# Two weight copies placed ahead of the small steps of a unit in ScalarE's queue

## The chip, the cores and the metric

The kernel runs on one core of a Trainium2 chip, in one launch. The metric is the device time of that core in microseconds. Three timed executions of the kernel before took 2869.0, 2869.91 and 2870.35 us; the median is 2869.91 us. PE is TensorE (PEld its weight loads), ACT is ScalarE, DVE is VectorE, POOL is GpSimd, SP is SyncE, which issues the weight DMAs.

## The reference

Two layers run one after the other over 256 tokens of width 2048, all in float32. The first takes 16 meta tokens ahead of them. It is a normed input projection, stick-breaking attention with 8 heads, a pool over trailing windows of 2, 4, 8 and 16 tokens, two gated projections back to 2048, and an output projection. The second is a hybrid mixer (chunked retention with 8 heads, gated delta rule with 16 heads), cross attention to 256 memory tokens, and a feed-forward block of width 8192.

```
h = rmsnorm(x); zin = h @ w_in                       # 2048 x 10240
y = sigmoid(m_attn) * (o_attn @ w_attn_up) + sigmoid(m_pool) * (o_pool @ w_pool_up)
x = rmsnorm(x + y @ w_out)
x = x + hybrid_mixer(rms_norm(x))                    # conv of 4 taps, silu, l2 norm, delta rule
x = x + cross_attention(rms_norm(x), rms_norm(mem))
x = x + square(relu(rms_norm(x) @ w_ff1)) @ w_ff2
```

For a pair of delta-rule heads the mixer projects queries, keys and values, runs a convolution of four taps over the tokens, applies silu, scales queries and keys to length one, inverts a triangular matrix of 64 by 64 per chunk, and passes a state through the chunks.

## The kernel before, in words

**Units.** All weights lie in one array of 471 units of 128 x 2048 floats (1 MB each; some are shorter). A unit passes three stations. SP loads it into one of three raw buffers. ACT copies it, rounded to float32r, into one of three `whi` buffers. DVE subtracts the copy from the raw weights into one of three `wlo` buffers. TensorE multiplies high part and low part with the likewise split activations. Copy and subtraction are made in two halves, (j, 0) and (j, 1), and so are the unit's matmuls, `("mm", (j, 0))` and `("mm", (j, 1))`. A high copy of unit j waits for the raw load, and for `w_used` of unit j - 3, that is for the last matmul of the unit that held the same `whi` buffer (`s_hi`, line 1698; the copy is line 1704). The subtraction is `s_lo` (line 2068, by the helper in line 2042). Every matmul stands in line 1346 (line 1349 the transposes), so that one goes by tiles in the trace.

**The written order.** `make_plan` writes one list of steps; each engine's program walks it and emits the steps that it has a part in, in the list's order. So the list is the order of each engine's queue, and an instruction that waits holds up all behind it on its engine. `hi_to(n)`, `lo_to(n)` and `load_to(n)` add high copies, low parts and loads up to unit n if they are not in the list yet. `SPL` and `RAW` are 3.

**A unit's steps.** `unit()` (line 236) adds, for unit j: low parts of the next units and the high copies of unit j + 2 where they are missing; the first half's matmuls; a `slot()` where the stage has `half=True`; a low half; the second half's matmuls; the reading of a finished sum (`last()`, where a pair of units ends); a `slot()`; and the second low half of unit j + 2. The high copies of unit j + 3 come at the start of the next call, so behind the slot at the end of unit j. A unit that is `lazy`, the last before the input of the matmuls changes, leaves its last low half to the next.

**Slots.** `slot()` moves every running task by one step. The tasks are generators: attention heads (`g_att`), norm factors of the second layer (`g_factors`, line 611), retention heads (`g_ret`, `g_rtr`), convolutions (`g_conv`, line 756), delta-rule head pairs (`g_gdn`, line 796), cross attention (`g_x`), transposes (`g_xt`). A step has parts on several engines. Those that the prediction speaks of are:

- `cvs`: ACT makes the sigmoid of a convolution's result (line 1900); DVE multiplies with it in `cvq`; ACT squares the product (line 1905) and rounds the square to `cacc_r` (line 1907).
- `cvl`: DVE makes the low part `t` of the squares. `cvn`: TensorE sums both over the head, `cacc_r` first, then `t`; ACT takes Ln and Exp of the sum (`rsqrt`, lines 1739 and 1741).
- `g_up` and `g_down`, five times by turns for block sizes 2 to 32: TensorE multiplies, DVE copies to `Cm`; TensorE multiplies, ACT copies to `TT` (line 1929), DVE transposes `TT` to `Tn` (line 2556). `g_up64` and `g_down64` end the inversion. `g_v` and `g_o` follow, with DVE copying to `U` (line 2613).
- `a2`: ACT copies and DVE subtracts the merged activations for the output projection of the first layer (lines 1795 and 2042). They stand between two units.
- `mixf`, `fin tok`, `fin n1`: a TensorE sum, Ln and Exp on ACT (two functions, each with its table load), and four DVE operations.
- `att_z`, `att_e`, `att_o`: the attention scores, the weights (an Exp on ACT, line 1777, and then masks on POOL, line 2784), and the product with the values.

In the delta-rule stage a slot stands in the middle and at the end of each unit. One head pair has 10 units: two each for queries, keys and values, and four for a gate. The inversion of pair h runs beside the convolutions of pair h + 1. For pairs 1 to 7 `g_down` falls in the middle of units and `g_up` at their ends. Pair 0 has one `yield` more (`if h == 0: yield`), and there `g_down` falls at the ends and `g_up` in the middle.

Of the kernel before, what the change touches and what calls it, by code (L numbers as in the profile page):

```python
# [161 lines left out]
class Plan:  # L162
# [9 lines left out]
    def add(self, stage, key, **values):  # L172
        self.steps.append((stage, key))
        self.at[stage, key] = values
        return values


RAW, SPL = 3, 3
# [3 lines left out]
def make_plan():  # L182
# [8 lines left out]
    def load_to(n):  # L191
        while done["load"] < min(n, len(units)):
            j = done["load"]
            done["load"] += 1
            add("load", j)

    def hi_to(n):
        while done["hi"] < min(n, len(units)):
            j = done["hi"]
            done["hi"] += 1  # L200
            load_to(j + 1)
            for k in range(2):
                add("hi", (j, k))

    def lo_to(n):
        while done["lo"] < min(n, 2 * len(units)):
            j, k = divmod(done["lo"], 2)
            done["lo"] += 1
            hi_to(j + 1)
            add("lo", (j, k))  # L210
            if k == 1:
                load_to(j + 1 + RAW)
# [3 lines left out]
    def slot():  # L216
        for g in list(tasks):
            if next(g, "end") == "end":
                tasks.remove(g)
# [16 lines left out]
    def unit(half=False, hooks={}, lazy=False, first=None, last=None):  # L236
        j = done["unit"]
        done["unit"] += 1
        lo_to(2 * (j + SPL - 1))
        hi_to(j + SPL)  # L240
        if (j, 0) in hooks:
            hooks[j, 0]()
        add("mm", (j, 0))
        if (j, 1) in hooks:
            hooks[j, 1]()
        if half:
            slot()
        lo_to(2 * (j + SPL) - 1)
        add("mm", (j, 1))
        if first:  # L250
            first()
        if last:
            last()
        slot()
        if not lazy:
            lo_to(2 * (j + SPL))
# [5 lines left out]
    def pair(kind, tag, ready, evac, half=False, lazy=False, hooks={}, defer=False):  # L262
        p = begin(kind, tag, ready)
        full = done["unit"] + p["nu"]

        def read():
            name, value = evac(tag, p["idx"], p["bank"], full)
            main.free(p["bank"], name, value)

        for k in range(p["nu"]):  # L270
            end = k == p["nu"] - 1
            unit(half, hooks, lazy and end, read_late if k == 0 else None, (lambda: waiting.append(read)) if end and defer else read if end else None)

    def turns(kind, two, ready, half=False, hooks={}):

        ps = [(begin(kind, tag, ready), evac) for tag, evac in two]
        full = done["unit"] + 3

        def read(n):
            def f():  # L280
                p, evac = ps[n]
                name, value = evac(p["tag"], p["idx"], p["bank"], full + n)
                main.free(p["bank"], name, value)
            return f

        for k in range(4):
            unit(half, hooks, first=read_late if k == 0 else None, last=read(k - 2) if k > 1 else None)
# [2673 lines left out]
```

## Time and profile before

| | |
|---|---|
| median of 3 executions | 2869.91 us (2869.0 to 2870.35) |
| profiled execution, span from first to last instruction | 2866.7 us |
| PE busy | 2829.8 us (99%) |
| DVE busy | 1931.7 us (67%) |
| ACT busy | 1355.2 us (47%) |
| POOL busy | 57.2 us (2%) |
| granted TensorE clock, mean | 0.999 |
| HBM read | 499.95 MB, 175 GB/s |

The profiled execution is known by its span; what the device time has beside a span is the 3.2 us between 2866.7 and the median. A busy time adds the durations of an engine's instructions without counting an overlap twice. The ends of matmuls are modelled, so that an idle time of PE is the least that it can have been.

### The profile page before, as it was taken

To read this page: it belongs to the slowest core of one execution; us is meant where nothing else is said; L and a number is where in the kernel's file an instruction comes from. 1 tells how busy PE (TensorE), PEld (TensorE's weight loads), DVE (VectorE), ACT (ScalarE), POOL (GpSimd) and SP (SyncE) were. 2 spreads that over 40 slices of the span, in tenths; PEclk is the share of its full clock that TensorE was granted. 3 is DMA by queue.
4 is the path that set the end of the run, shared out by engine and by line. 5 is a ranking of instruction groups with operands and counts; after the bars stand their busy time and mean duration, and the time that the engine had idled before them with its cause. 6 is when DMAs were issued, how large, how long until landed. Compare 5 with 4: busy or idle time off the path is not lost.

```text
span 2866.7 us, 38752 instructions
## 1 busy us (share of the span) xinstructions
PE 2829.8 (99%) x15872; PEld 2442.7 (85%) x15872; DVE 1931.7 (67%) x2513; ACT 1355.2 (47%) x1729; POOL 57.2 (2%) x102
## 2 busy tenths in 40 slices
PE   9999999999999999999999999999999999999998
PEld 8899888888888888888888888888888888888887
DVE  7645557678766658888888875456666655566556
ACT  5433654357443446555555543444345434444434
POOL 0000210000000000000000000000000000000000
PEclk9999999999999999999999999999999999999999
DMA  7444444564555544334343455544354454554453
GB/s 278 183 184 162 143 166 185 197 231 177 197 184 193 204 151 162 141 139 147 133 145 123 145 175 192 187 182 162 146 200 182 178 204 182 200 200 182 186 196 147
DMA packets 72849, 506.66 MB, mean 177 GB/s; under 512 B 8384, under 2 KB 8512, under 8 KB 12896
## 3 DMA queue, kind: packets, MB, share of 16 engines
q1 hardware_dynamic: 71136, 497.83, 46.9%
q0 software_dynamic: 1104, 5.90, 0.6%
q8 instruction: 126, 2.06, 0.3%
q10 hardware_dynamic: 432, 0.45, 0.0%
q14 instruction: 51, 0.42, 0.0%
HBM read 499.95 MB, written 2.10 MB: 175 GB/s over the span
## 4 chain that ended last, share of the span: by engine, by line
PE 86%; DVE 9%; ACT 3%; issue 2%; DMA 1%; SPq 0%; DVEq 0%; POOL 0%; ACTq 0%
PE double L1346 80%; PE bank L1346 5%; DVE cacc L2048 2%; DVE wlo L2042 2%; ACT whi L1704 1%; DVE cst L2065 1%; PE bank L1349 1%; DVE cacc L2045 1%; ACT L1900 0%; DVE Tn L2556 0%; DVE cst L2042 0%; DVE Cm L2042 0%; ACT tmp L1905 0%; DMA vec<-in_vec 0%; DMA raw<-in_wall 0%
## 5 line engine op out<-in xcount | busy, mean ns | idle before, releaser
L1346 PE MATMUL double<-AA,whi 128*128 128x512 f32 (+1 forms) x5008 | 1643.1, 380 | 3.5 <-DVE wlo L2042 3.3
L1346 PE MATMUL double<-AA,wlo 128*128 128x256 f32 (+1 forms) x4624 | 1297.0, 281 | 0.0
L1704 ACT ACTIVATE whi<-raw 128x1024 fp32r<-128x1024 f32 x926 | 925.2, 1049 | 780.3 <-PE double L1346 748.5
L2042 DVE TENSOR_TENSOR wlo<-raw,whi 128x1024 fp32r<-128x1024 f32 (+1 forms) x934 | 1101.7, 1214 | 229.9 <-ACT whi L1704 227.6
L1346 PEld LDWEIGHTS double<-AA,whi 128*128 128x128 f32 x5008 | 915.9, 188 | 181.2 <-DVE wlo L2042 5.2
L1346 PEld LDWEIGHTS double<-AA,wlo 128*128 128x128 f32 x4624 | 874.7, 189 | 1.5
L1346 PE MATMUL double<-whi,AA 128*128 128x512 f32 x1536 | 487.9, 393 | 0.5 <-DVE wlo L2042 0.5
L1346 PEld LDWEIGHTS double<-whi,AA 128*128 128x128 f32 x1536 | 288.5, 188 | 61.0 <-DVE wlo L2042 1.3
L1346 PE MATMUL double<-whi,BB 128*128 128x512 f32 x1024 | 316.8, 389 | 0.0
L1346 PE MATMUL double<-wlo,AA 128*128 128x512 f32 x768 | 299.1, 389 | 0.0
L1346 PEld LDWEIGHTS double<-whi,BB 128*128 128x128 f32 x1024 | 192.2, 188 | 40.1
L1346 PE MATMUL double<-wlo,BB 128*128 128x512 f32 x512 | 199.3, 389 | 0.0
L1346 PEld LDWEIGHTS double<-wlo,AA 128*128 128x128 f32 x768 | 144.4, 188 | 28.7
L2065 DVE TENSOR_REDUCE tmp<-double 128x512 f32<-128x1024 f32 x60 | 73.4, 1224 | 133.1 <-PE double L1346 133.1
L1346 PEld LDWEIGHTS double<-wlo,BB 128*128 128x128 f32 x512 | 96.1, 188 | 19.8
L2042 DVE TENSOR_TENSOR XT<-double,XT 128x512 f32<-128x512 f32 x64 | 41.3, 686 | 93.0 <-PE double L1346 93.0
L1980 ACT ACTIVATE tmp<-tmp 128x512 f32<-128x512 f32 x32 | 20.2, 633 | 172.1 <-DVE tmp L2048 172.1
L1346 PE MATMUL double<-BB,whi 128*128 128x512 f32 x256 | 90.0, 394 | 0.0
L2048 DVE SCALAR_TENSOR_TENSOR cacc<-cst,vec,cacc 128x256 f32<-128x256 f32 x144 | 69.8, 485 | 5.1
L1346 PE MATMUL double<-BB,wlo 128*128 128x256 f32 x256 | 71.6, 280 | 0.0
L2042 DVE TENSOR_TENSOR X<-double,X 128x512 f32<-128x512 f32 x48 | 33.2, 691 | 53.4 <-PE double L1346 52.5
L2042 DVE TENSOR_TENSOR BB<-tmp,BB 128x512 fp32r<-128x512 f32 x40 | 27.7, 693 | 49.5 <-ACT BB L1753 49.5
(335 smaller groups left out, 1722.2 us busy)
## 6 DMA issues: line engine op xcount, KB each, us to landing
raw<-in_wall SPq DMA_DIRECT2D x462, 1024.0 KB, 4.8
raw<-in_wall SPq DMA_DIRECT2D x9, 256.0 KB, 6.7
X<-in_xT SPq DMA_DIRECT2D x1, 2048.0 KB, 11.4
Mm<-in_memT POOLq DMA_DIRECT2D x1, 2048.0 KB, 15.5
tmp<-rqk POOLq DMA_DIRECT2D x16, 128.0 KB, 2.2
mblk<-in_memT SPq DMA_DIRECT2D x8, 256.0 KB, 4.5
dec<-in_dec POOLq DMA_DIRECT2D x1, 1536.0 KB, 8.6
hs<-in_hsT SPq DMA_DIRECT2D x4, 272.0 KB, 5.2
```

The costliest lines, as they stand in the source:

```text
L1346: return q.matmul(out, lhsT, rhs, start=start, stop=stop, skip_group_check=True)
L1349: return q.transpose(out, in_, C("ident") if ident is None else ident)
L1704: q.activation(hi_of(j)[:, c], raw[j % RAW][:, c], ACT.Copy).then_inc(S("w_hi"), 1)
L1980: q.activation(x, x, ACT.Square).then_inc(S("f_act"), 1)
L2042: return q.tensor_tensor(out, a, b, o)
L2045: return q.tensor_scalar(out, a, s, None, o)
L2048: return q.scalar_tensor_tensor(out=out, in0=a, scalar=s, in1=b, op0=o0, op1=o1)
L2065: q.reduce_sum(out, both, mybir.AxisListType.X).then_inc(S("sum"), 1)
```

## The change

In `unit()`, for all but the lazy units, the high copies of unit j + 3 are now written ahead of the slot at the end of unit j, behind the reading of a finished sum. Before, they were written behind this slot, at the start of the next unit's call. Nothing is added to or taken from any engine, and no wait changes its target.

```
--- before.py
+++ after.py
@@ -251,6 +251,8 @@
             first()
         if last:
             last()
+        if not lazy:
+            hi_to(j + 1 + SPL)
         slot()
         if not lazy:
             lo_to(2 * (j + SPL))
```

## Rows read from the trace of the kernel before

**Rows 1.** The page's busy line: busy us, share, instructions.
```profile
PE 2829.8 (99%) x15872; PEld 2442.7 (85%) x15872; DVE 1931.7 (67%) x2513; ACT 1355.2 (47%) x1729; POOL 57.2 (2%) x102
```
**Rows 2.** Windows: stretch, its us, busy (instructions) of PE, PEld, DVE, ACT, POOL.
```profile
1180.00:1650.00 470.00, 457.48 (x2804) 382.05 (x2804) 400.04 (x683) 250.63 (x378) 16.18 (x21) 1.00 0.39 139
...
2190.00:2857.00 667.00, 667.00 (x3375) 569.93 (x3374) 398.55 (x404) 282.24 (x318) 0.00 (x0) 1.00 0.49 186
```
**Rows 3.** Timeline of ACT, queries' convolution: start, us, instruction, idle and releaser.
```profile
1453.87 0.64 ACT L1900 ACTIVATE tmp<-cacc 128x512 f32<-128x512 f32 x1 [3.72 <-DVE cacc L2048]
1456.17 0.63 ACT L1905 ACTIVATE tmp<-qkvq 128x512 f32<-128x512 f32 x1 [1.67 <-DVE qkvq L2042]
1456.83 0.63 ACT L1907 ACTIVATE cacc_r<-tmp 128x512 fp32r<-128x512 f32 x1
1457.37 1.99 ACT L1704 ACTIVATE whi<-raw 128x1024 fp32r<-128x1024 f32 x2
1459.27 0.55 ACT L1929 ACTIVATE TT<-bank 64x128 f32<-64x128 f32 x2
```
**Rows 4.** Timeline of DVE in the same head pair.
```profile
1459.85 0.91 DVE L2556 STREAM_TRANSPOSE Tn<-TT 64x256 f32<-64x256 f32 x2 [2.58 <-ACT TT L1929]
...
1475.13 0.67 DVE L2042 TENSOR_TENSOR t<-tmp,cacc_r 128x512 fp32r<-128x512 f32 x1
1476.06 1.23 DVE L2042 TENSOR_TENSOR wlo<-raw,whi 128x1024 fp32r<-128x1024 f32 x1 [0.26 <-ACT whi L1704]
...
1486.77 0.41 DVE L2613 COPY U<-bank 128x256 f32<-128x256 f32 x1
```
**Rows 5.** Timeline of ACT, keys' convolution of that pair.
```profile
1471.03 1.28 ACT L1900 ACT_TABLE_LOAD   x1 [4.64 <-DVE cacc L2048]
1472.32 0.63 ACT L1900 ACTIVATE tmp<-cacc 128x512 f32<-128x512 f32 x1
1473.78 0.63 ACT L1905 ACTIVATE tmp<-qkvk 128x512 f32<-128x512 f32 x1 [0.83 <-DVE qkvk L2042]
```
**Rows 6.** Timeline of PE where that pair's delta rule goes on.
```profile
1487.33 0.46 PE L1346 MATMUL bank<-U,cross 128*128 128x128 f32 x2 [0.60 <-DVE U L2613]
```
**Rows 7.** Timeline of ACT beside the inversion of head pair 0.
```profile
1152.32 0.63 ACT L1900 ACTIVATE tmp<-cacc 128x512 f32<-128x512 f32 x1 [5.26 <-DVE cacc L2048]
1152.86 0.55 ACT L1929 ACTIVATE TT<-bank 64x128 f32<-64x128 f32 x2
...
1169.34 0.55 ACT L1929 ACTIVATE TT<-bank 64x128 f32<-64x128 f32 x2
```
**Rows 8.** Timeline of PE: the end of the inversion of head pair 0.
```profile
1170.03 0.65 PE L1346 MATMUL bank<-TT,Mf 64*64 64x64 f32 x8 [0.67 <-ACT TT L1929]
```
**Rows 9.** Timeline of PE: the norm sum of pair 0's keys.
```profile
1103.32 0.47 PE L1346 MATMUL bank<-cacc_r,ones_r 128*128 128x512 f32 x1 [1.48 <-ACT cacc_r L1907]
```
**Rows 10.** Timeline at the second layer's start, ACT: Exp of `fin n1`.
```profile
708.42 0.42 ACT L1741 ACTIVATE rs__123<-rs__123 128x256 f32<-128x256 f32 x1
```
**Rows 11.** The same stretch, DVE: first operation of `fin n1`.
```profile
709.01 0.42 DVE L2099 TENSOR_SCALAR nacc__124<-bank 128x256 f32<-128x256 f32 x1
```
**Rows 12.** The same stretch, PE: second half of unit 116.
```profile
712.91 0.50 PE L1346 MATMUL double<-whi,AA 128*128 128x512 f32 x1 [0.52 <-DVE wlo L2042]
```
**Rows 13.** Timeline at the first layer's output projection, ACT: seven `a2` copies.
```profile
592.22 3.75 ACT L1795 ACTIVATE AA<-Macc 128x512 fp32r<-128x512 f32 x7
```
**Rows 14.** The same stretch, DVE: seven `a2` low parts.
```profile
592.86 4.30 DVE L2042 TENSOR_TENSOR AA<-Macc,AA 128x512 fp32r<-128x512 f32 x7
```
**Rows 15.** The same stretch, PE: the output projection's first matmul.
```profile
594.97 0.39 PE L1346 MATMUL double<-AA,whi 128*128 128x512 f32 x1
```
**Rows 16.** Timeline of POOL: attention weights masked; three of eight lie like this one.
```profile
332.47 0.69 POOL L2784 TENSOR_SCALAR_AFFINE_SELECT att<-att 128x128 f32<-128x128 f32 x3 [9.64 <-ACT att L1777]
```
**Rows 17.** Timeline of PE: the product with the values that waits for them.
```profile
335.73 0.97 PE L1346 MATMUL bank<-att,v 128*128 128x256 f32 x6
```

More of the change, by code:

```diff
@@ L253, in unit @@
             last()
+        if not lazy:
+            hi_to(j + 1 + SPL)
         slot()
```

## The prediction

> **What bounds the kernel now.** I read the page's busy line first: TensorE is busy 2829.8 of 2866.7 us, no other engine over 67% [rows 1]. A change of order on ScalarE can therefore only give back TensorE's 36.9 us of idle time, or add to it. So I looked for where they lie, with windows by stage. The feed-forward stage has none: TensorE is busy 667.00 of 667.00 us [rows 2]. The delta-rule stretch from 1180 to 1650 us holds 12.5 (470.00 less 457.48) [rows 2]; the rest is at the kernel's start and end and in a handful of places at changes of stage. Then I went through the waits of TensorE and the timelines of the delta-rule stretch. Each of the six head pairs whose convolutions (of pairs 2 to 7) run beside an inversion shows the same five late places in the side steps: the operand `TT` of `g_up`, `t` of `cvn`, `Cm`, `Ce`, and `U` of `g_o`, the last one with 0.60 us idle [rows 6]. What is late there is VectorE: from the reading of the queries' sum to that copy of `U` it has no pause but one of 2.58 us, where it waits for ScalarE's `TT` [rows 4], and some under 0.7 us. ScalarE is slow with `TT` because it stands behind a pair of high copies, and these behind the square and the rounding of `cvq` [rows 3]. In this stretch the order on ScalarE decides, though it is busy only about half of the time.
>
> **The change part by part.** The edit moves a pair of high copies; it adds no instruction. The two copies hold ScalarE for 1.90 us (1457.37 to 1459.27, when the next begins) [rows 3]. Its DMAs stay where they are: `hi_to` asks for a load that the list already has, so nothing moves past SP's queue, and POOL's has no part in it. The copy's own wait, for the last matmul of unit j, is met about when the slot begins, so what is queued behind it (the end-of-unit steps on ScalarE, and VectorE and TensorE that wait for these) is late by at most the 1.90 us, unless a table load had stood hidden in an idle stretch. At most unit ends ScalarE has no step between the two places: there nothing changes, and that is the whole feed-forward stage after its first units, the memory keys and nearly all of the output projections.
>
> *Head pairs with conv 2 to 7, six times.* Now the sigmoid starts at 1453.87, the square waits for VectorE until 1456.17, and the copies follow behind both. With the change the copies follow the sigmoid (next instruction 0.54 behind a start, as from 1456.83 to 1457.37): 1454.41 to 1456.31. The square then starts at 1456.31, the rounding 0.66 later, `TT` at 1457.51 in place of 1459.27 [rows 3]. The copies use a pause, and VectorE goes on 1.76 us earlier. In the keys' convolution the same move costs: the sigmoid would start 1.76 earlier, at 1470.56, the copies run from 1471.10 to 1473.00, and the square starts at 1473.00, 0.78 earlier than now [rows 5]; so does the rounding, and `t` on VectorE, 1474.35 for 1475.13. Behind it the low part no longer waits 0.26 for its high copy (its start lies 0.93 behind that of `t`; I take 0.61 without the wait, with some launch time): 1474.96 for 1476.06 [rows 4]. From there to the copy to `U` at 1486.77 VectorE has no pause, so `U` and TensorE's `g_o` come 1.10 earlier [rows 4, 6]. Gain 6 x 1.10 = 6.6 us. Bounds: 0, if the keys' part takes all back, and 6 x 1.76 = 10.6, if it takes nothing; 12.5 is all the idle time [rows 2]. I take 1.10, which is chained from adjacent rows.
>
> *Head pair 0, inversion beside conv 1.* Here `g_down` falls at ends of units, so its `TT` copies come behind the moved copies. At 1152.86 `TT` stands directly behind the sigmoid [rows 7]; it gets 1.90 us later, and VectorE, with no pause until the last `TT`, with it. Two `TT` before it lose 1 us each in idle stretches of VectorE and leave about 0.3 (estimate from the same timeline). At 1169.34 the same happens again: the sigmoid is late by 2.2, and the copies come in between: 1.90 more [rows 7]. TensorE takes that `TT` at 1170.03 with 0.67 idle already [rows 8], so it passes all of it on: 0.3 + 1.90 + 1.90 = +4.1 us. Bounds: 1.9 (only the last one counts) and 4.1.
>
> *Conv 0, no inversion beside it.* The square now starts 1.46 us behind the sigmoid's start [rows 5]; with copies between, 0.54 + 1.90 = 2.44. Each `cacc_r` is 0.98 later. The queries' delay passes on some 0.7 (less the 0.26 for the low part), the keys' adds 0.98: +1.7. TensorE already waits 1.48 us for the keys' `cacc_r` [rows 9], so it is paid in full. Bounds 1.0 and 2.0.
>
> *Start of the second layer.* `fin n1` stands at the end of unit 114: its Exp ends at 708.84 [rows 10] and VectorE takes it up at 709.01 [rows 11]. With the copies of unit 117 ahead it ends at 710.74; VectorE starts at 710.78, 1.77 later, and the low part behind it is the one that TensorE waits for at 712.91 with 0.52 idle [rows 12]. So +1.8. `mixf` one unit before is late by as much, but VectorE then waits for `fin tok` anyway, whose end doesn't move. Bounds 0 and 1.8.
>
> *First layer's output projection.* The seven `a2` copies begin at 592.22 [rows 13] and would begin at 594.12. The first low part, now 592.86 and one seventh of 4.30 long, so ready by 593.55 with its tail [rows 14], would be ready at 595.45, with some 0.1 to the matmul 595.55; TensorE wants it at 594.97 [rows 15]. +0.6. Bounds 0 and 1.0.
>
> Sum: 0.6 + 1.8 + 1.7 + 4.1 - 6.6 = +1.6 us on the profiled 2866.7. The median lies 3.2 above this span; I carry the difference over: 2869.91 + 1.6 = 2871.5 us.
>
> *What the rest hides.* The attention weights of three heads come 1.9 later: masked by 333.16 now [rows 16], by 335.06 then, and TensorE takes them at 335.73 [rows 17], 0.67 left. In the other heads a table load that now runs in an idle stretch would come behind the copies, and the delay stays under that. The norm factors of cross attention and feed-forward come up to 2.6 us later (1.9, and part of a table load that is now hidden), with VectorE's low parts behind them still a few tenths before their matmuls. If that cover is too thin, it is a few tenths at each.
>
> One page speaks against the change. The row shows a table load of 1.28 us and the sigmoid 1.29 behind the load's start [rows 5]: nothing else is paid. The Trainium skill ("ScalarE: Activation LUTs", What ACT_TABLE_LOAD costs) states that a switch costs about 2.66 us, since a drain of 1.38 comes with the load. By that, copies that are now put directly ahead of table loads would make those dearer, at the second layer's start by some 2.8 us (estimate from the page) for two loads. No row here shows such a drain, also where a load follows the copies at once, and I leave it out.
>
> **The rivals.**
> *The gain stays, the losses are covered (faster).* If pair 0, conv 0 and the stage changes find slack that I don't see, 2869.9 - 6.6 = 2863.3 us. For it: VectorE is busy 67% over the whole kernel [rows 1]. Against: TensorE already idles at three of those places [rows 8, 9, 12].
> *The keys' convolution takes the gain back (slower).* Place: the copies between sigmoid and square of `cvq` for the keys. Price: all of the 6.6, so 2869.9 + 8.2 = 2878.1 us. It decides from the point where the square comes 1.10 us later than worked out, that is where the launch behind the copies, or a late `w_used`, holds ScalarE so long. For it: the same order costs 0.98 in conv 0. Against: the sum leaves 1.10 by rows that hold to 0.1 us.
> *The order doesn't matter.* ScalarE is busy 47% [rows 1] and buffers two units ahead, so that all is hidden: 2869.9 us. Against: the late `TT` of [rows 3, 4] stands directly behind the copies.
>
> **How the numbers follow.** Forecast 0.62, with 2869 to 2874 as its own range; order without effect 0.12; faster rival 0.12; slower rival 0.14. A measurement of this kernel can tell about 0.2%, 5.7 us, from no change. The forecast and the third rival lie within it, the other two lie mostly beyond: faster 0.10, same 0.77, slower 0.13. The range leaves out a tenth on each side: 2864.5 to 2877.
>
> **What would show it.** Right: in pairs 2 to 7 the `TT` at the old 1459.27 comes behind the rounding, VectorE's pause of 2.58 falls under 1, the period from one pair to the next gets about 1.1 us shorter, and only the wait for `U` stays. In pair 0 TensorE's wait for `TT` ahead of `g_up64` grows from 0.67 to some 3 us, another of about 1.2 appears two units before, the waits for `cacc_r` grow to about 1.7 and 2.4, and that at 712.91 to 2.3. Wrong: if the periods of the six pairs don't move, if pair 0 shows no longer wait, or if waits appear in attention, retention or feed-forward, where I have none.

## The result and the profile after

The changed kernel takes 2873.65 us (median of 16 runs, 2872.17 to 2876.23), the kernel before on the same chip 2868.83 us (16 runs): ratio 1.0018, 95% interval [1.0011, 1.0025]. That is some 5 us more: less than the 0.2% that the prediction took as telling, but the interval lies above 1, so the kernel is slower by a little. The span went from 2866.7 to 2871.2 us. In the profile's lines those of the changed kernel stand two further down than those of before (L1348 is the matmul, L1706 the high copy, L1931 the copy of `TT`). One of the eleven executions of e4_norm below is a slow one (3763.02 us, granted clock 0.695), which its ratio leaves out and its median doesn't.

The busy line of after, against [rows 1]: the span is 4.5 us longer, TensorE's busy time 4.4. So the idle time of TensorE is the same (37.0 for 36.9 us), and a change that adds no instruction made its busy time longer. Some 3 of the 4.4 us are matmuls at a lower granted clock, as shown below; the rest is scattered, 0.6 of it in the first 40 us, where it doesn't move the time.
```profile
PE 2834.2 (99%) x15872; PEld 2446.3 (85%) x15872; DVE 1929.8 (67%) x2513; ACT 1357.2 (47%) x1729; POOL 57.4 (2%) x102
```
TensorE's waits after (operand and releaser: us in total, times, longest):
```profile
PE bank L1348 <- ACT TT L1931: 6.3, 3, 3.3
PE bank L1348 <- DVE U L2615: 5.1, 12, 0.9
PE double L1348 <- DVE wlo L2044: 5.1, 6, 2.3
PE bank L1348 <- ACT cacc_r L1909: 2.1, 2, 1.6
PE bank L1348 <- DVE Cm L2044: 2.1, 2, 1.9
PE bank L1348 <- DVE qx L2044: 1.4, 1, 1.4
```
The same view of before:
```profile
PE bank L1346 <- ACT TT L1929: 4.7, 8, 1.7
PE bank L1346 <- DVE U L2613: 4.0, 6, 0.9
PE bank L1346 <- DVE Cm L2042: 3.8, 7, 1.9
...
PE bank L1346 <- DVE t L2042: 3.3, 8, 0.5
PE bank L1346 <- ACT cacc_r L1907: 2.0, 2, 1.5
PE bank L1346 <- DVE Ce L2045: 1.3, 6, 0.2
```
Many small waits have gone (in the six head pairs all those for `TT`, `t`, `Cm` and `Ce`, six of each), and a few long ones have come. Totals hide that: `TT` went from eight waits to three, and from 4.7 to 6.3 us. `U` has a second, small wait in each of the six pairs.

**In the six head pairs** ScalarE does what was worked out. The queries' convolution that answers to [rows 3]:
```profile
1461.70 0.63 ACT L1902 ACTIVATE tmp<-cacc 128x512 f32<-128x512 f32 x1 [3.71 <-DVE cacc L2050]
1462.24 1.99 ACT L1706 ACTIVATE whi<-raw 128x1024 fp32r<-128x1024 f32 x2
1464.14 0.61 ACT L1907 ACTIVATE tmp<-qkvq 128x512 f32<-128x512 f32 x1
1464.78 0.64 ACT L1909 ACTIVATE cacc_r<-tmp 128x512 fp32r<-128x512 f32 x1
1465.32 0.55 ACT L1931 ACTIVATE TT<-bank 64x128 f32<-64x128 f32 x2
```
`TT` begins 3.62 us behind the sigmoid, where it was 5.40. VectorE, against [rows 4], and TensorE, against [rows 6]:
```profile
1465.90 0.91 DVE L2558 STREAM_TRANSPOSE Tn<-TT 64x256 f32<-64x256 f32 x2 [0.79 <-ACT TT L1931]
...
1482.11 0.69 DVE L2044 TENSOR_TENSOR t<-tmp,cacc_r 128x512 fp32r<-128x512 f32 x1 [0.86 <-ACT cacc_r L1909]
...
1493.41 0.42 DVE L2615 COPY U<-bank 128x256 f32<-128x256 f32 x1
```
```profile
1486.28 0.68 PE L1348 MATMUL bank<-U,cross 128*128 128x128 f32 x4 [0.20 <-DVE U L2615]
...
1493.98 0.46 PE L1348 MATMUL bank<-U,cross 128*128 128x128 f32 x2 [0.62 <-DVE U L2615]
```
The pause of 2.58 is 0.79 now; the keys' edit makes one of 0.86 at `t`. From the queries' sigmoid to the late `U` it is 31.71 us, where it was 32.90.

**In head pair 0** (against [rows 7, 8]) the copies stand between the sigmoid and `TT`, and TensorE waits twice. ScalarE first, then TensorE:
```profile
1176.78 0.63 ACT L1902 ACTIVATE tmp<-cacc 128x512 f32<-128x512 f32 x1
1177.31 1.99 ACT L1706 ACTIVATE whi<-raw 128x1024 fp32r<-128x1024 f32 x2
1179.20 0.55 ACT L1931 ACTIVATE TT<-bank 64x128 f32<-64x128 f32 x2
```
```profile
1161.57 0.65 PE L1348 MATMUL bank<-TT,Mn 128*64 128x64 f32 x8 [1.38 <-ACT TT L1931]
...
1179.89 0.65 PE L1348 MATMUL bank<-TT,Mf 64*64 64x64 f32 x8 [3.27 <-ACT TT L1931]
```
**At the second layer's start** (against [rows 10 to 12]), ScalarE and then TensorE:
```profile
705.99 1.99 ACT L1706 ACTIVATE whi<-raw 128x1024 fp32r<-128x1024 f32 x2
708.00 1.28 ACT L1741 ACT_TABLE_LOAD   x1
709.29 0.47 ACT L1741 ACTIVATE rs__123<-bank,con 128x256 f32<-128x256 f32 x1
709.79 1.28 ACT L1743 ACT_TABLE_LOAD   x1
711.08 0.42 ACT L1743 ACTIVATE rs__123<-rs__123 128x256 f32<-128x256 f32 x1
```
```profile
715.44 0.50 PE L1348 MATMUL double<-whi,AA 128*128 128x512 f32 x1 [2.28 <-DVE wlo L2044]
```
And one wait is in none of the terms: the norm of cross attention reaches `qx` late.
```profile
1971.31 3.69 PE L1348 MATMUL bank<-mblk,qx 128*128 128x256 f32 x16 [1.39 <-DVE qx L2044]
```

**The granted clock.** Windows of after behind three of these waits (after the busy times: granted clock, DMA share, GB/s):
```profile
714.00:720.00 6.00, 4.56 (x13) 3.61 (x14) 5.96 (x10) 0.00 (x0) 0.27 (x1) 0.72 0.47 175
1094.00:1100.00 6.00, 5.38 (x19) 4.41 (x20) 5.40 (x9) 4.81 (x6) 0.00 (x0) 0.72 0.48 175
...
1180.00:1186.00 6.00, 6.00 (x34) 4.99 (x34) 4.78 (x7) 2.09 (x3) 0.00 (x0) 0.72 0.48 175
```
Of the two levels, 1.2 and 2.4 GHz, the lower holds for a part of these six us; all matmuls there are busy time, but some take twice as long (0.79 us where the same form took 0.39, in e2_pair0 behind the wait in pair 0). Apart from the last 4 to 7 us of the kernel, where every trace has the lower level, before has one such stretch of its own, behind its two waits in the last head pair, and after has none there:
```profile
1674.00:1680.00 6.00, 6.00 (x32) 5.10 (x32) 5.57 (x12) 1.96 (x3) 0.00 (x0) 0.72 0.50 178
```

Each matmul of after set against the same one of before, in the two profiled executions, gives the account (change of the shift, us). The lower clock is counted net of what a later wait takes up:

| place | predicted | measured |
|---|---|---|
| `a2`, at 594.97 | +0.6 | +0.6 |
| `fin n1`, at 712.91 | +1.8 | +1.8 |
| lower clock behind it | none | +1.3 |
| conv 0 | +1.7 | +1.7 |
| pair 0, its two waits | +4.1 | +4.3 |
| lower clock behind them | none | +1.6 |
| six head pairs | -6.6 | -7.2 |
| last pair: before's lower clock is absent | none | -1.6 |
| `qx`, at 1966.91 | none | +1.8 |
| sum (with +0.2 of rest) | +1.6 | +4.5 |

### The profile page after: what moved, and what is told of

The parts are those of the page before. It is cut to its first block and busy times, and to the rows that moved or that the text cites. A ratio compares the mean times of both kernels' runs of the same rounds, so it can differ in the third digit from the quotient of the medians.

```text
span 2871.2 us, 38752 instructions
## 1 busy us (share of the span) xinstructions
PE 2834.2 (99%) x15872; PEld 2446.3 (85%) x15872; DVE 1929.8 (67%) x2513; ACT 1357.2 (47%) x1729; POOL 57.4 (2%) x102
## 5 line engine op out<-in xcount | busy, mean ns | idle before, releaser
L1348 PE MATMUL double<-AA,whi 128*128 128x512 f32 (+1 forms) x5008 | 1644.9, 380 | 3.4 <-DVE wlo L2044 2.8
L1706 ACT ACTIVATE whi<-raw 128x1024 fp32r<-128x1024 f32 x926 | 926.7, 1049 | 966.8 <-PE double L1348 908.3
L1348 PE MATMUL double<-AA,wlo 128*128 128x256 f32 (+1 forms) x4624 | 1298.4, 281 | 0.0
L1348 PEld LDWEIGHTS double<-AA,whi 128*128 128x128 f32 x5008 | 917.0, 188 | 181.9 <-DVE wlo L2044 4.8
L1348 PEld LDWEIGHTS double<-AA,wlo 128*128 128x128 f32 x4624 | 876.3, 190 | 1.5
L1348 PE MATMUL double<-whi,AA 128*128 128x512 f32 x1536 | 488.9, 394 | 2.3 <-DVE wlo L2044 2.3
L1348 PEld LDWEIGHTS double<-whi,AA 128*128 128x128 f32 x1536 | 289.4, 188 | 61.9 <-DVE wlo L2044 2.7
L1348 PE MATMUL double<-whi,BB 128*128 128x512 f32 x1024 | 316.9, 389 | 0.0
L1348 PE MATMUL double<-wlo,AA 128*128 128x512 f32 x768 | 299.9, 390 | 0.0
L1348 PEld LDWEIGHTS double<-whi,BB 128*128 128x128 f32 x1024 | 192.3, 188 | 40.1
L1348 PE MATMUL double<-wlo,BB 128*128 128x512 f32 x512 | 199.4, 389 | 0.0
L1348 PEld LDWEIGHTS double<-wlo,AA 128*128 128x128 f32 x768 | 144.8, 189 | 29.1
L1348 PEld LDWEIGHTS double<-wlo,BB 128*128 128x128 f32 x512 | 96.1, 188 | 19.8
L1348 PE MATMUL double<-BB,whi 128*128 128x512 f32 x256 | 90.0, 394 | 0.0
L1348 PE MATMUL double<-BB,wlo 128*128 128x256 f32 x256 | 71.6, 280 | 0.0
```

The costliest lines, as they stand in the source:

```text
L1348: return q.matmul(out, lhsT, rhs, start=start, stop=stop, skip_group_check=True)
L1706: q.activation(hi_of(j)[:, c], raw[j % RAW][:, c], ACT.Copy).then_inc(S("w_hi"), 1)
```

## The experiments

A variant limits the new lines to some units (a condition on `j`); the rest stays as before. Ratios are to the kernel before on the same chip; 0.001 is 2.9 us.

| run | units with the edit, other edits | median us | ratio, 95% |
|---|---|---|---|
| e1_pairs | 197 to 252 | 2862.36 | 0.9972 [0.9963, 0.9982] |
| e2_pair0 | 187 to 192 | 2875.47 | 1.0023 [1.0014, 1.0032] |
| e3_start | 114 | 2871.64 | 1.0011 [1.0002, 1.0020] |
| e4_norm | 306, 338 | 2871.04 | 1.0006 [0.9997, 1.0016] |
| e5_start_fill | 114, filler | 2870.25 | 1.0007 [0.9998, 1.0016] |
| e6_not_keys | as e1, keys' units left out | 2859.43 | 0.9970 [0.9959, 0.9982] |
| e7_keys | the keys' units of e1 alone | 2872.64 | 1.0015 [1.0006, 1.0024] |
| e8_no_yield | all, pair 0 a half unit earlier | 2867.36 | 1.0000 [0.9991, 1.0009] |
| e9_pair0_fill | 187 to 192, filler | 2871.33 | 1.0010 [1.0001, 1.0019] |
| e10_conv0 | 178 to 182 | 2870.47 | 1.0006 [0.9997, 1.0015] |
| e11_best | as e6, filler | 2857.97 | 0.9961 [0.9949, 0.9974] |
| e12_best_keys0 | as e11, and 180 to 182 | 2858.11 | 0.9964 [0.9950, 0.9977] |

**Where the gain and the losses lie.** One place alone in each of four runs.
```
-        if not lazy:
+        if not lazy and 197 <= j <= 252:      # e1_pairs
+        if not lazy and 187 <= j <= 192:      # e2_pair0
+        if not lazy and j == 114:             # e3_start
+        if not lazy and j in (306, 338):      # e4_norm
```


> The copies are ahead of the slot in units 197 to 252 alone, the six head pairs with convolutions 2 to 7. Theory (each pair's gain is local: ScalarE copies in a pause, VectorE goes on earlier): the six pairs gain 7.5 us in the trace of the full change, 1.25 each, so the kernel takes 7 to 9 us less than the one before (ratio 0.9970 to 0.9975). Rival (the six pairs only make up what pair 0 had lost before them): alone they have nothing to make up, and the time stays within 2 us of the kernel before.

> The copies are ahead of the slot in units 187 to 192 alone, beside the inversion of head pair 0. Theory: two late TT copies, TensorE's waits of 1.55 and 3.44 us in place of 0.83, and a stretch of matmuls at a lower granted clock behind the longer wait: +5.5 to +6 us on the span. Rival (the two waits alone, as forecast): +4.1 us and the clock at 1.00 behind the wait.

> The copies are ahead of the slot in unit 114 alone, so that only fin n1 at the second layer's start comes behind them. Theory (a longer wait of TensorE, and then a lower granted clock for some matmuls): the wait before the second half of unit 116 grows by 1.8 us, and +1.5 us come behind it at the lower clock: +3.3 us in all. Rival (the slow matmuls come from something else in the full change, the delay of mixf in unit 113 or the earlier weight copies): +1.8 us and no lower clock.

> The copies are ahead of the slot in units 306 and 338 alone, ahead of the norm factors of cross attention and feed-forward. Theory: the factor's Exp ends about 2.6 us later, VectorE reads and scales the second query sum later, and TensorE's first score matmul waits for it: +1.5 to +1.7 us, all of it at that place (about 1967 us), and nothing at the feed-forward's start. Rival (the forecast's: a few tenths, hidden by the low parts' lead): under +0.5 us.

By the ratios: -8.0, +6.6, +3.2 and +1.7 us. With e10_conv0's +1.7 (below) and 0.6 for `a2`, which had no run of its own, the sum is +5.8, where the whole change shows +5.2. Each of these has an interval of some 2.7 us to either side, and those of e4_norm and e10_conv0 take in no change; so the sum alone proves little. The traces are sharper. By the shifts of the matmuls the places are -7.2 (e1_pairs), +5.9 with the lower clock (e2_pair0), +3.1 with the lower clock (e3_start), +1.8 (e4_norm), +1.7 (e10_conv0) and +0.6 (`a2`), together +5.9; after has +4.5, and +6.1 without the stretch of lower clock that only before has in the last pair. The parts add up and don't share a cost. e4_norm's trace has the wait for `qx` with the same 1.39 us as after, and nothing at the feed-forward stage, so the full change's missed term is this one place.

**The keys' units.** Of the units of the six pairs those with `j % 10 == 1` have the copies between the sigmoid and the square of the keys.
```
+        if not lazy and j in range(197, 253) and j % 10 != 1:   # e6_not_keys
+        if not lazy and j in range(197, 253) and j % 10 == 1:   # e7_keys
```


> As the run with units 197 to 252, but in the first value unit of each head pair (unit 201, 211, ... 251: the slot with the keys' cvq) the copies stay behind the slot as before. Theory (the queries' place gains 1.76 us per pair, and the keys' place gives part of it back): VectorE keeps the full 1.76, and the kernel takes 9 to 11 us less than before, 2 to 3 less than with the keys' place moved too. Rival (U is bound by something else in the second half of a pair): the same as with the keys' place moved, 7 to 9 us less.

> Only in units 201, 211, ... 251 are the copies ahead of the slot (the keys' cvq of conv 2 to 7). Theory: the square comes about 1.0 us later behind the copies, less 0.3 that the low part no longer waits, so each pair is longer by 0.3 to 0.7 us: +2 to +4 us. Rival (the keys' place costs nothing by itself, since VectorE is the late one there): within 1 us of the kernel before.

The keys' edit costs, with or without the other: +4.3 us by the ratio alone (+3.6 by its matmuls), and 3.5 us by which e6_not_keys' matmuls have gained more over the six pairs than those of e1_pairs (by ratios, 0.9970 and 0.9972, the two can't be told apart). In e7_keys `t`, `Cm` and `Ce` are late as before and a new wait for `U` is added:
```profile
1462.31 0.50 PE L1348 MATMUL bank<-t,ones_r 128*128 128x512 f32 x1 [0.49 <-DVE t L2044]
...
1473.34 0.65 PE L1348 MATMUL bank<-Ce,Tn 64*64 64x64 f32 x8 [0.22 <-DVE Ce L2047]
1481.01 0.68 PE L1348 MATMUL bank<-U,cross 128*128 128x128 f32 x4 [0.21 <-DVE U L2615]
```
In e6_not_keys only the last `U` is left of a pair's waits:
```profile
1482.39 0.46 PE L1348 MATMUL bank<-U,cross 128*128 128x128 f32 x2 [0.58 <-DVE U L2615]
```
Its six pairs are 10.7 us shorter than before's (e1_pairs' 7.2 and these 3.5), 1.78 us each; the prediction had worked out 1.76 for the queries' part before the keys' took from it. By its ratio the run gains 8.6 us, a little under the 9 to 11 expected, with an interval that takes them in.

**Pair 0's beat.** In pair 0 an extra `yield` puts its down steps at the ends of units, where the moved copies stand. Here the full change is kept and the `yield` left out.
```
-        if h == 0:
-            yield
```


> The full change, and head pair 0 without its extra step of delay ahead of the inversion, so that its g_down falls in the middle of units as in all other pairs. Theory (pair 0 lost because its TT copies came behind the weight copies): its two waits for TT (1.55 and 3.44 us) and the slow stretch behind them go, and pair 0 behaves as the others: 5 to 7 us less than the full change, so 0 to 2 us under the kernel before. Rival (pair 0 loses since conv 1 and the inversion are late on VectorE whatever the parity): the time stays at that of the full change.

The time is 5.2 us under the full change by the ratios (6.1 by the spans, of which 5.1 lie between conv 0 and the end of the six pairs), and no step of pair 0's inversion waits; this is the step that met the copies in after:
```profile
1171.13 0.67 PE L1346 MATMUL bank<-TT,Mf 64*64 64x64 f32 x8
```
So pair 0's cost is the meeting of two things, not the copies as such. In this run a wait as long as after's at 712.91 (2.24 us) is followed by no lower clock; its window of 714 to 720 us shows:
```profile
714.00:720.00 6.00, 4.22 (x18) 3.49 (x19) 5.97 (x10) 0.00 (x0) 0.00 (x0) 1.00 0.48 169
```
**Does the wait cost the clock?** Matmuls of constants that nobody reads are put in TensorE's queue ahead of the one that waits, sized to end as the operand comes.
```
+            if key == (7, 4):          # also in g_down; h == 0 in g_up64; ahead of (116, 1)
+                for _ in range(8):
+                    mm_group(bank[r["b1"]][:, 0:128], C("ident"), C("upto"))
```


> As the run with unit 114 alone, and TensorE has ten small float32 matmuls of 128 columns (ident by upto, into a free bank that nothing reads) in front of the second half of unit 116, where it would otherwise wait some 2.4 us. Theory (the clock falls because TensorE stands idle): the filler keeps it busy, it takes no time of its own since the low part comes at the same moment, the granted clock stays at 1.00 and 1.5 us of the 3.3 come back: +1.8 us on the kernel before. Rival (the slow matmuls behind the wait come from the traffic of loads and copies there): they stay slow, +3.3 us.

> The edit stands only at units 187 to 192 (head pair 0), and fourteen 128-column matmuls of constants stand in TensorE's queue before pair 0's first 64-wide update, where the edit without them (run before as e2_pair0) waited longest (about 3.4 us); they take 2.39 us per ten, so about 3.3 us, and end as the awaited operand comes. Theory (the longer wait costs itself once, and the lower granted clock after it costs about 1.5 us more): the time is 1.0 to 1.8 us under e2_pair0's, about +5 us on the kernel before by its profiled span +6.3 instead of +7.7, and the granted clock stays 1.00 over the 8 us behind the wait. Rival (the slower matmuls behind the wait are not due to the idle engine but to the weights or operands they read): the matmuls behind it are slow again and the time is e2_pair0's or above it.

TensorE at the second layer's start in e5_start_fill; the filler of 2.39 us lies where the wait was, and the matmul behind it is 1.6 us later than before (it shifts by 1.8 there, as in e3_start):
```profile
712.10 2.39 PE L1351 MATMUL bank<-con 128*128 128x128 f32 x20
714.50 0.50 PE L1351 MATMUL double<-whi,AA 128*128 128x512 f32 x1
```
The window 714 to 720 us, e3_start, then e5_start_fill:
```profile
714.00:720.00 6.00, 4.89 (x14) 3.93 (x15) 5.97 (x9) 0.00 (x0) 0.60 (x2) 0.72 0.48 175
```
```profile
714.00:720.00 6.00, 6.00 (x29) 4.73 (x27) 5.96 (x9) 0.78 (x1) 1.03 (x2) 1.00 0.55 184
```
In pair 0 the window 1174 to 1180 us, e2_pair0, then e9_pair0_fill:
```profile
1174.00:1180.00 6.00, 3.56 (x17) 3.09 (x18) 3.65 (x6) 3.53 (x6) 0.00 (x0) 0.73 0.17 22
```
```profile
1174.00:1180.00 6.00, 5.94 (x46) 5.15 (x45) 3.64 (x6) 3.53 (x6) 0.00 (x0) 1.00 0.07 14
```
The same operands and the same delay, without the idle time: the clock stays at its upper level, and in e9_pair0_fill the matmuls behind the wait come 1.6 us earlier than in e2_pair0, in e5_start_fill 1.3 us less late than in e3_start. The ratios say the same with the places mixed in: 1.0023 falls to 1.0010 (some +2.9 us on before, where about +5 was expected; the spans give +4.8), 1.0011 to 1.0007. The mean granted clock is known for every execution: e9_pair0_fill 0.999 in all eleven, e2_pair0 0.997 in eight of ten and 0.998 in two. That is more than pair 0's one stretch can make: in the profiled executions e2_pair0 has a second stretch, in the last head pair, that e9_pair0_fill has not, and why it is missing there isn't shown. At the second layer's start one trace with the filler stands against a clock that fell in two of three without it; alone it would prove little. The rival, that the matmuls are slow for the operands they read, is out: e9_pair0_fill reads the same ones, and e8_no_yield reads those of the second layer's start behind a wait of 2.24 us, both at the upper level.

**Conv 0, and the best version.**
```
+        if not lazy and 178 <= j <= 182:                          # e10_conv0
+        if not lazy and (j in range(197, 253) and j % 10 != 1 or 180 <= j <= 182):   # e12
```


> The edit stands only at units 178 to 182 (convolution 0, query and key). Prediction on record: +1.7 us from the longer waits for the norm's accumulation. Theory now, from the full change's trace: the query's wait grows by 1.0 us, the lower clock behind it may cost 1.5 us, the key's wait shrinks by 0.8 us: between +0.2 and +1.8 us. Rival (the key's part costs as well): +2.5 us or more.

> The edit at the units of e6_not_keys (197 to 252 but for those of the key's convolution), and eight 128-column matmuls of constants before each of the two TensorE waits of 1.9 and 2.1 us in the last head pair (its update and its down step of width 4), which the kernel before has too. Each group of eight takes about 1.9 us, no more than the wait. Theory (a stretch of lower clock behind such a wait costs 1.5 us, and work in place of the wait keeps the clock): 1 to 1.8 us under e6_not_keys, thus about 0.9965 of the kernel before, granted clock 1.00 over the stretch of the two waits. Rival (the filler delays the matmuls behind it, or the clock falls all the same): at e6_not_keys or above it.

> As e11_best, with the edit at units 180 to 182 (the key's part of convolution 0) too. Theory (the key's wait for its accumulation shrinks from 1.6 to 0.8 us there): 0.8 us under e11_best. Rival (only the shift made by the query's part made the key's wait shorter): the same as e11_best or up to 1 us over it.

e10_conv0 measures +1.7 us. TensorE's two waits for `cacc_r`, first e10_conv0, then e12_best_keys0:
```profile
1090.99 0.47 PE L1348 MATMUL bank<-cacc_r,ones_r 128*128 128x512 f32 x1 [1.56 <-ACT cacc_r L1909]
1105.38 0.47 PE L1348 MATMUL bank<-cacc_r,ones_r 128*128 128x512 f32 x1 [0.59 <-ACT cacc_r L1909]
```
```profile
1089.74 0.47 PE L1348 MATMUL bank<-cacc_r,ones_r 128*128 128x512 f32 x1 [0.54 <-ACT cacc_r L1915]
1104.48 0.47 PE L1348 MATMUL bank<-cacc_r,ones_r 128*128 128x512 f32 x1 [2.50 <-ACT cacc_r L1915]
```
My reading that the keys' wait "shrinks" by the keys' part was wrong. By itself that part makes the wait 1.02 us longer (2.50 for 1.48 [rows 9]). It is short in e10_conv0 and in after since TensorE arrives late, by the query's 1.0 and 1.6 us of lower clock; the keys' operand then sets the time at +1.7 all the same. That is the sum of the rows without any lower clock (0.7 and 0.98), so here it seems to cost nothing: the next wait takes it up. No trace has the queries' edit with the clock at its upper level there, to show it directly. e12_best_keys0 is not 0.8 us faster than e11_best but level; its 1 us is made up in its profiled execution by a stretch of lower clock that e11_best has behind that wait and it has not.

e11_best takes 2857.97 us, 11 us under before and about 1.5 under e6_not_keys by the medians (intervals overlap; by the spans 2.0, of which 1.7 are gained in the last head pair). Its window 1660 to 1666 us, e6_not_keys' and then its own:
```profile
1660.00:1666.00 6.00, 4.07 (x25) 3.37 (x25) 5.94 (x13) 2.83 (x7) 0.00 (x0) 0.91 0.20 85
1666.00:1672.00 6.00, 6.00 (x34) 5.07 (x34) 5.55 (x12) 2.01 (x2) 0.00 (x0) 0.80 0.49 178
```
```profile
1660.00:1666.00 6.00, 5.99 (x45) 5.33 (x44) 5.94 (x12) 2.49 (x7) 0.00 (x0) 1.00 0.17 68
1666.00:1672.00 6.00, 6.00 (x46) 5.07 (x44) 5.70 (x11) 2.01 (x2) 0.00 (x0) 1.00 0.48 175
```
It beats both kernels, before and after.

## Why the prediction was right, and where not

The forecast was 2871.5 us and no change to be told; the median is 2873.65, inside its own range of 2869 to 2874, but near its top. The mechanism held at every place that had a term; that the total stayed in the range is in part luck. The forecast had +1.6 us, the medians of the 16 runs differ by 4.8, and the starting point of 2869.91 lay 1.1 above that of the 16 runs, which hid a part of the miss.

- *Six head pairs, 1.10 us each*: right, slightly small. The sigmoid, the copies, the square, the rounding and `TT` follow in the order and at the distances worked out (3.62 for a predicted 3.64). The bound of 1.76 for the queries' part alone is what e6_not_keys measures. After gains 1.20 each, which is what the `U` chain gives by itself (1.19). "Only the wait for `U` stays" is nearly right; a small second one came, of 0.20 here.
- *Pair 0, +4.1*: right as to the idle time (+4.3; the wait of 3.27 was forecast at about 3, that of 1.38 at 1.2). The term lacked what follows the idle time, +1.6.
- *Conv 0, +1.7*: right in sum (+1.7 in after and alone). The waits were forecast as 1.7 and 2.4 and are 1.56 and 0.58: I let TensorE arrive at the second 0.7 us later than before, and it arrives 2.6 later, by 1.0 of longer wait and 1.6 of lower clock.
- *Second layer's start, +1.8*: right (+1.8, wait 2.28 for a forecast 2.3), and again without the clock, +1.3.
- *`a2`, +0.6*: right by the trace; no run tests it alone.
- *"The norm factors of cross attention ... come up to 2.6 us later ... a few tenths"*: the step that failed. The cover was judged by the low parts behind the norm; but VectorE itself waits for the factor (4.64 us, until 1961.10, in after), multiplies `qx` with it behind those low parts, and the first memory matmul waits for `qx`: +1.8, and alone +1.8 in e4_norm's trace (its ratio, 1.0006, can't tell it from nothing). TensorE has no wait for `qx` in the kernel before, and I took that for a cover of the whole delay without following the chain through `qx`.
- *Table loads*: rightly left without a drain. Behind the copies at the second layer's start the load takes 1.28 us and the activation starts 1.29 behind the load's start, as in [rows 5]. The Trainium skill ("ScalarE: Activation LUTs", What ACT_TABLE_LOAD costs) has 2.66 us for a switch, drain included. This trace doesn't agree: behind 90 of the 105 loads of after the next instruction starts 1.29 to 1.30 us behind the load's start.

Of the rivals, "losses are covered" is out (e2_pair0, e3_start and e10_conv0 each pay in full in their traces), "order doesn't matter" is out (e1_pairs: 0.9972), and "the keys' convolution takes the gain back" is real with 3.5 us, near the 0.66 per pair that stood in the sum, but not the whole gain. The net came near no change since a gain of 8 us and losses of 14 us (the ratios of the parts) happened to stand close; the forecast of 1.6 was short by the 1.8 of `qx` and a net 1.3 of clock in the profiled executions, less 0.6 that the six pairs gain beyond their term.

## What to carry to other kernels

An order on an engine that is half idle is worth what it does to the one step that the bounding engine waits for, and that differs by place: list every place where something stands behind the moved instructions, price each alone, and apply the edit only where it pays. Here a rule for all units made the kernel 0.2% slower, and the same edit at the units of one stage but for every tenth one made it 0.3% faster. Price a wait of the bounding TensorE at more than its length: count the slower matmuls that may follow it, and whether a later wait takes them up.

## What the runs showed of the hardware

Behind TensorE's waits the granted clock fell in some executions and not in others, with the same wait at the same place. Over the profiled executions of all fourteen kernels it fell behind ten of fourteen waits at conv 0's keys or queries (1.47 us and more), seven of twelve pairs of waits in the last head pair (about 1.7 and 1.9 us), two of three at 712.91 (about 2.3) and both at pair 0's update (3.27 us); behind none of the six waits of about 1.4 us at `TT` and `qx`, and at none of the six fillers (e5_start_fill, e9_pair0_fill, two each in e11_best and e12_best_keys0). Each fall cost 1.3 to 1.6 us net where no later wait took it up. Over 16 runs the changed kernel has a mean granted clock of 0.997 (two 0.998, eleven 0.997, three 0.996), and these groups' mean times are 2872.8, 2873.8 and 2875.3 us: 2.5 of the runs' spread of 4.1 us. What decides whether the clock falls behind a given wait stays open.
